# Attention over wide tiles: the next pair's scores issued behind the values instead of ahead of the transposes

## The chip, the cores and the metric

The kernel runs on one NeuronCore of a Trainium2 chip. The metric is the device time of one execution in microseconds (us), lower is better. Three runs of the kernel before took 2337.08, 2338.13 and 2340.18 us; their median, 2338.13 us, is the time before.

## The reference, cut to what matters

One layer of a hybrid block on x of shape (1, 1024, 1024): a norm, an input projection, then two groups of heads side by side (sparse attention with top-k keys, and an mLSTM), an output projection, and a mixture of 32 experts. The change touches only the attention:

```python
idx_score = where(admissible, idx_score, -inf)
_, sel = lax.top_k(idx_score, k_sel)                      # 256 keys of each query
logits = einsum('bqgrd,bqkgd->bqgrk', qb, ks) * scale     # 8 heads of 64, 2 key/value heads
logits = where(valid, logits, -inf)
p = softmax(logits)
out = einsum('bqgrk,bqkgd->bqgrd', p, vs)
```

## The kernel before, in words

Everything before the attention writes what it needs: `q_hi`/`q_lo` and `k_hi`/`k_lo` (float32 split in two parts, so that three fast products replace one exact one), `vtok` (the values) and `score`, which by then holds 0 for a chosen key and a very negative number for every other. The kernel gathers nothing: it computes scores over all keys of the causal prefix and adds that mask.

The attention has 8 tiles of 128 queries. Tile i has w = 128·(i+1) keys, so that tiles 0 to 3 have at most 512 (the constant `NARROW` is 4) and tiles 4 to 7 have 640, 768, 896 and 1024; the text calls the first four narrow and the others wide. Each tile has 8 heads. A unit u is one head of one tile (u = 0 to 63, tile u // 8), and TensorE works on units in pairs u, u+1. For a unit the stages are:

- **scores** (PE, `scores(u)`, L1573 to L1589): one call does both units of a pair; unit u writes PSUM banks 0 and 1 and u+1 banks 2 and 3. It waits until the masks of the preceding pair have read those banks (`v_msk`, L1577).
- **mask** (DVE, L2034 to L2044): adds the mask, copies to `a_s` and takes the row's maximum; L2046 makes the exponential's bias of it.
- **exp** (ACT, L1227 to L1236): exponential of `a_s` into `a_p`, with the row sum.
- **normalize** (DVE, L2007 to L2014): a reciprocal of the sum (L2011) and a multiplication of `a_p` by it (L2014). DVE's own order is mask u, mask u+1, normalize u, normalize u+1 (L2031 to L2049).
- **transposes** (PE, L1631 to L1641): i+1 blocks of `a_p` into PSUM. For narrow tiles the result has a bank for even and one for odd units (L1638); for wide tiles it takes the two banks 4 and 5 together, so that one unit's transposes must have been copied out before the next unit's begin (L1637).
- **copy out** (ACT, `pt_out`, L1238 to L1245): PSUM to `a_t`, which has three slots. ACT's own order is pt_out(u), exp(u+2), pt_out(u+1), exp(u+3) (L1250 to L1253).
- **values** (PE, L1643 to L1653): one call per pair, into banks 6 or 7.

Every engine runs its instructions in the order in which the program gives them. The order on PE is written out by hand in the loop at L1656 to L1665. Four side operations are put between these on ACT and DVE: `q_hi_of` (L1161, ACT, behind exp(u+2) at the third unit of a tile), `q_lo_of` (L2021, DVE, between the masks of the seventh and eighth unit), `mx_hi_of` (L1225, ACT, behind exp(40) and exp(48)) and `mx_lo_of` (L2028, DVE, behind the mask of unit 48). `at_out` (L1054, ACT) copies a finished tile. Behind the attention PE goes on with the output projection (L1431 to L1433).

Of the kernel before, what the change touches and what calls it, by code (L numbers as in the profile page):

```python
# [35 lines left out]
NT = T // P  # L36
# [4 lines left out]
HEADS, HD, KVH = 8, 64, 2  # L41
NARROW = 512 // P
# [299 lines left out]
def build(nc, I, out):  # L342
# [4 lines left out]
    with ExitStack() as ctx:  # L347
# [222 lines left out]
        def pair(b):  # L570

            return ps[:, b:b + 2, :].rearrange("p b n -> p (b n)")
# [27 lines left out]
        def head(u):  # L600

            k = u % HEADS
            return 4 * (k % 2) + k // 2
# [832 lines left out]
        def _(pe):  # L1436
# [136 lines left out]
            def scores(u):  # L1573
                i = u // HEADS
                w = P * (i + 1)
                if u >= 2:
                    pe.wait_ge(s.v_msk, u)  # L1577
                if u % HEADS == 0:
                    pe.wait_ge(s.v_qklo, i + 2)
                for a in range(0, w, 512):  # L1580
                    b = min(a + 512, w)
                    for n, (q_, k_) in enumerate(((q_hi, k_hi), (q_hi, k_lo), (q_lo, k_hi))):
                        for e in range(2):
                            h = head(u + e)
                            rows = slice(HD * (h // 4), HD * (h // 4) + HD)
                            m = nc.tensor.matmul(pair(2 * e)[:, a:b], q_[rows, i % 2, h % 4, :], k_[rows, a:b],
                                                 start=(n == 0), stop=(n == 2))
                            if n == 2 and b == w:
                                m.then_inc(s.p_s, 1)  # L1589
# [41 lines left out]
            def transposes(u):  # L1631
                pe.wait_ge(s.v_arow, u + 1)
                narrow = u // HEADS < NARROW
                if narrow and u >= 2:
                    pe.wait_ge(s.a_pt, u - 1)
                if not narrow:
                    pe.wait_ge(s.a_pt, u)  # L1637
                dst = ps[:, 4 + u % 2, :] if narrow else pair(4)  # L1638
                for j in range(u // HEADS + 1):
                    m = nc.tensor.transpose(dst[:, j * P:(j + 1) * P], a_p[:, u % 2, j * P:(j + 1) * P], ident)  # L1640
                m.then_inc(s.p_pt, 1)  # L1641

            def values(u):  # L1643
                i, j = u // HEADS, u % HEADS // 2
                pe.wait_ge(s.a_pt, u + 2)
                if j == 0 and i >= 2:
                    pe.wait_ge(s.a_at, i - 1)
                for b in range(i + 1):
                    for e in range(KVH):
                        rows = slice(HD * e, HD * e + HD)  # L1650
                        m = nc.tensor.matmul(ps[rows, 6 + i % 2, j * P:(j + 1) * P], vtok[:, b, rows], a_t[:, (u + e) % 3, b, :],  # L1651
                                             start=(b == 0), stop=(b == i), skip_group_check=True)
                m.then_inc(s.p_pv, 1)  # L1653

            pe.wait_ge(s.a_mt, NT)
            for u in range(0, NT * HEADS, 2):  # L1656
                if u + 2 < NT * HEADS:
                    scores(u + 2)
                transposes(u)
                if u // HEADS < NARROW:  # L1660
                    transposes(u + 1)
                if u >= 2:
                    values(u - 2)
                if u // HEADS >= NARROW:
                    transposes(u + 1)  # L1665
            values(NT * HEADS - 2)
            pe.wait_ge(s.g_wolo, 2 * KC)
# [753 lines left out]
```

## Time and profile before

| | |
|---|---|
| median of three runs | 2338.13 us |
| the profiled execution, its own time | 2340.59 us |
| its span in the profile | 2338.8 us |
| PE busy | 2166.9 us (93%) |
| DVE busy | 1836.9 us (79%) |
| ACT busy | 1365.3 us (58%) |
| POOL busy | 560.8 us (24%) |
| mean granted TensorE clock | 0.951 |

The profiled execution is one more run; its own time is 1.8 us over its span, for what lies around it. The attention runs from 513 to 662 us of the span. In timelines, a line is: start, length, engine, line of the kernel, operation, what is written and read, and how often; brackets hold the idle time of the engine before it and the instruction that ended it. Lengths of successive PE lines overlap a little, since matmuls are pipelined; from one start to the next is the real pitch. The granted clock is 1.00 at 2.4 GHz and 0.50 at 1.2 GHz.

### The profile page before, as it was taken

What the parts mean: (1) busy time and instruction counts of PE and PEld (TensorE: products, weight loads), DVE (VectorE), ACT (ScalarE), POOL (GpSimd) and SP (SyncE); (2) the same over time, 40 slices, a digit from 0 to 9 for tenths busy, and PEclk for the clock granted to TensorE, in tenths of its full rate; (3) what the DMA queues carried; (4) which work ended last, traced back from release to release, by engine and by line L of the source; (5) the groups of instructions that cost most, each with busy time, mean ns of one, the idle gap of its engine ahead of it and who ended that gap; (6) DMA issues with size and microseconds to landing.
All of it is one profiled execution on the core that took longest, in us unless ns stands there. A gap on an engine that the chain in (4) does not pass through costs nothing.

```text
span 2338.8 us, 41558 instructions
## 1 busy us (share of the span) xinstructions
PE 2166.9 (93%) x15487; PEld 1731.9 (74%) x15487; DVE 1836.9 (79%) x2152; ACT 1365.3 (58%) x1545; POOL 560.8 (24%) x434
## 2 busy tenths in 40 slices
PE   6899999868899399999999999999999999999994
PEld 5677888645778377778778778778778778778773
DVE  3699999948733767877877877877877877877886
ACT  4542223875742457667667667667667667667665
POOL 1007786665000112112112112112112112112120
PEclk9769999967999699999999999999999999999997
DMA  5011211021023379889889889889889889889897
GB/s 142 19 46 37 55 46 49 29 66 44 1 93 118 105 261 341 311 287 349 309 284 349 310 285 349 313 285 351 309 286 347 313 285 347 311 285 347 315 370 260
DMA packets 253598, 526.46 MB, mean 225 GB/s; under 512 B 33048, under 2 KB 59800, under 8 KB 253180
## 3 DMA queue, kind: packets, MB, share of 16 engines
q1 hardware_dynamic: 240268, 483.27, 57.6%
q0 software_dynamic: 13264, 42.34, 7.5%
q8 instruction: 38, 0.62, 0.1%
q14 instruction: 28, 0.23, 0.0%
HBM read 490.96 MB, written 35.91 MB: 225 GB/s over the span
## 4 chain that ended last, share of the span: by engine, by line
PE 69%; DMA 10%; DVE 9%; ACT 5%; issue 4%; POOL 2%; SPq 0%; DVEq 0%; ACTq 0%; POOLq 0%
PE ps L1763 13%; PE ps L1765 12%; PE ps L1764 12%; DMA e_raw<-in_w_gate_up_dram 9%; PE ps L1770 9%; PE ps L1431 5%; PE ps L1432 5%; PE ps L1433 5%; DVE e_wlo L2262 2%; PE ps L1775 1%; PE ps L1506 1%; PE ps L1651 1%; PE ps L1640 1%; ACT a_p L1235 1%; DVE a_s L2040 1%
## 5 line engine op out<-in xcount | busy, mean ns | idle before, releaser
L1314 ACT ACTIVATE e_whi<-e_raw 128x2048 fp32r<-128x2048 f32 x411 | 785.8, 1917 | 421.5 <-PE ps L1765 313.4
L2262 DVE TENSOR_TENSOR e_wlo<-e_raw,e_whi 128x2048 fp32r<-128x2048 f32 x410 | 926.5, 2284 | 66.9 <-ACT e_whi L1314 65.3
L1763 PE MATMUL ps<-e_whi,xh 128*128 128x512 f32 x1088 | 434.7, 400 | 0.0
L1764 PE MATMUL ps<-e_whi,xl 128*128 128x512 f32 x1088 | 424.3, 390 | 0.0
L1765 PE MATMUL ps<-e_wlo,xh 128*128 128x512 f32 x1088 | 424.1, 390 | 0.0
L942 POOL DMA_INDIRECT x_d<-ym,scur x34 | 73.0, 2146 | 861.9 <-ACT ym L1347 841.5
L1763 PEld LDWEIGHTS ps<-e_whi,xh 128*128 128x128 f32 x1088 | 204.3, 188 | 52.7 <-issue 12.7
L1765 PEld LDWEIGHTS ps<-e_wlo,xh 128*128 128x128 f32 x1088 | 204.2, 188 | 44.0
L1763 PE MATMUL ps<-e_whi,ath 128*128 128x512 f32 x544 | 221.6, 407 | 13.1 <-DVE atl L2290 13.1
L1764 PEld LDWEIGHTS ps<-e_whi,xl 128*128 128x128 f32 x1088 | 204.5, 188 | 39.3
L1765 PE MATMUL ps<-e_wlo,ath 128*128 128x512 f32 x544 | 213.2, 392 | 0.0
L1764 PE MATMUL ps<-e_whi,atl 128*128 128x512 f32 x544 | 212.7, 391 | 0.0
L1431 PE MATMUL ps<-ht_hi,w_hi 128*128 128x512 f32 x416 | 168.8, 406 | 1.2 <-POOL w_lo L793 1.2
L2002 DVE MATCH_REPLACE8 score<-cols,score 128x384 f32<-128x384 f32 (+2 forms) x192 | 166.3, 872 | 0.0
L1433 PE MATMUL ps<-ht_hi,w_lo 128*128 128x512 f32 x416 | 164.3, 395 | 0.0
L1432 PE MATMUL ps<-ht_lo,w_hi 128*128 128x512 f32 x416 | 164.2, 395 | 0.0
L1998 DVE MAX8 cols<-score 128x8 f32<-128x384 f32 (+2 forms) x192 | 160.6, 876 | 0.0
L1763 PEld LDWEIGHTS ps<-e_whi,ath 128*128 128x128 f32 x544 | 102.5, 188 | 52.3 <-issue 33.7
L1770 PE MATMUL ps<-e_raw,xo 128*32 128x128 f32 x4096 | 125.6, 275 | 0.1
L1765 PEld LDWEIGHTS ps<-e_wlo,ath 128*128 128x128 f32 x544 | 102.5, 188 | 22.6
L1764 PEld LDWEIGHTS ps<-e_whi,atl 128*128 128x128 f32 x544 | 102.7, 189 | 18.6
L1770 PEld LDWEIGHTS ps<-e_raw,xo 128*32 128x32 f32 x4096 | 114.5, 111 | 0.6 <-issue 0.3
(351 smaller groups left out, 3348.8 us busy)
## 6 DMA issues: line engine op xcount, KB each, us to landing
e_raw<-in_w_gate_up_dram SPq DMA_DIRECT2D x275, 1024.0 KB, 6.7
e_raw<-in_w_down_dram SPq DMA_DIRECT2D x136, 1024.0 KB, 11.4
w_raw<-in_w_in_dram SPq DMA_DIRECT2D x20, 512.0 KB, 3.8
xt<-in_x_dram SPq DMA_DIRECT2D x8, 512.0 KB, 6.2
xr<-in_x_dram SPq DMA_DIRECT2D x8, 512.0 KB, 4.3
x_d<-x SPq DMA_DIRECT2D x8, 512.0 KB, 2.6
h_d<-h SPq DMA_DIRECT2D x8, 512.0 KB, 2.9
x<-x_d SPq DMA_DIRECT2D x8, 512.0 KB, 7.2
```

The lines of the kernel that those rows point to most:

```text
L942: nc.gpsimd.indirect_dma_start(x2_d[:, :], bass.IndirectOffsetOnAxis(ap=scur[:], axis=0), ym[:], None, compute_op=ALU.add).then_inc(s.st_y ...
L1314: nc.scalar.activation(e_whi[:, m % HRING, :], e_raw[:, m % RING, :], ACT.Copy).then_inc(s.e_hi, 1)
L1431: nc.tensor.matmul(dst, a_hi, b_hi, start=first, stop=False)
L1432: nc.tensor.matmul(dst, a_hi, b_lo, start=False, stop=False)
L1433: return nc.tensor.matmul(dst, a_lo, b_hi, start=False, stop=last)
L1763: nc.tensor.matmul(dst, a_hi, slot_hi, start=False, stop=False, skip_group_check=True)
L1764: nc.tensor.matmul(dst, a_lo, slot_hi, start=False, stop=False, skip_group_check=True)
L1765: return nc.tensor.matmul(dst, a_hi, slot_lo, start=False, stop=last, skip_group_check=True)
L1770: m = nc.tensor.matmul(ps[OVER * b:OVER * b + OVER, bank, 0:n], weights, moving[:, n * b:n * b + n], start=first, stop=last, skip_group_ch ...
L1998: nc.vector.max(top8[:, k, :], sc[k]).then_inc(s.v_topk, 1)
L2002: nc.vector.match_replace(sc[k], top8[:, k, :], sc[k], GONE).then_inc(s.v_topk, 1)
L2262: nc.vector.tensor_tensor(e_wlo[:, m % HRING, :], e_raw[:, m % RING, :], e_whi[:, m % HRING, :].bitcast(F32), ALU.subtract).then_inc(s.e_l ...
```

## The change

In the loop that orders PE's work, for pairs of wide tiles (u = 32 to 62) the call `scores(u + 2)` moves from ahead of `transposes(u)` to behind `values(u - 2)`. For narrow tiles the order stays.

```diff
             for u in range(0, NT * HEADS, 2):
-                if u + 2 < NT * HEADS:
+                narrow = u // HEADS < NARROW
+                if narrow and u + 2 < NT * HEADS:
                     scores(u + 2)
                 transposes(u)
-                if u // HEADS < NARROW:
+                if narrow:
                     transposes(u + 1)
                 if u >= 2:
                     values(u - 2)
-                if u // HEADS >= NARROW:
+                if not narrow and u + 2 < NT * HEADS:
+                    scores(u + 2)
+                if not narrow:
                     transposes(u + 1)
```

No instruction is added or removed, and no other engine's order is touched. The diff is complete.

## Rows read from the trace of the kernel before

**Rows 1.** Busy time by stretch: from, to, length, PE, PEld, DVE, ACT, POOL, PE clock, DMA
```profile
574.00:653.00 79.00, 71.93 (x769) 57.28 (x769) 62.22 (x163) 61.13 (x104) 0.00 (x0) 1.00 0.01 2
```
**Rows 2.** Waits, 574 to 653 us: engine, line, waited for; total us, times, longest
```profile
PE ps L1586 <- DVE cols L2040: 6.4, 10, 1.1
```
**Rows 3.** Timeline of PE, tile 7 (1024 keys), one pair and the next
```profile
648.48 0.50 PE L1586 MATMUL ps<-k_hi,q_hi 64*128 64x512 f32 x2
...
649.74 0.40 PE L1586 MATMUL ps<-k_hi,q_lo 64*128 64x512 f32 x2
650.07 1.09 PE L1640 MATMUL ps<-cst,a_p 128*128 128x128 f32 x8
651.09 1.97 PE L1651 MATMUL ps<-a_t,vtok 128*64 128x128 f32 x32
652.99 1.09 PE L1640 MATMUL ps<-cst,a_p 128*128 128x128 f32 x8
655.29 1.08 PE L1640 MATMUL ps<-cst,a_p 128*128 128x128 f32 x8 [1.21 <-DVE a_p L2014]
```
**Rows 4.** Timeline of DVE and ACT in the same stretch
```profile
651.53 1.22 DVE L2040 CUSTOM_DVE_ANT_0 a_s<-ps,score 128x1024 f32<-128x1024 f32 x1
...
654.13 1.02 ACT L1244 ACTIVATE a_t<-ps 128x1024 f32<-128x1024 f32 x1
```
**Rows 5.** Timeline of PE, tile 4 (640 keys), one pair
```profile
582.79 0.77 PE L1640 MATMUL ps<-cst,a_p 128*128 128x128 f32 x5
583.49 1.31 PE L1651 MATMUL ps<-a_t,vtok 128*64 128x128 f32 x20
584.73 0.76 PE L1640 MATMUL ps<-cst,a_p 128*128 128x128 f32 x5
585.67 0.50 PE L1586 MATMUL ps<-k_hi,q_hi 64*128 64x512 f32 x2 [0.18 <-DVE cols L2040]
...
586.64 0.28 PE L1586 MATMUL ps<-k_hi,q_lo 64*128 64x128 f32 x2
```
**Rows 6.** Timeline of DVE in the same stretch
```profile
583.77 0.82 DVE L2040 CUSTOM_DVE_ANT_0 a_s<-ps,score 128x640 f32<-128x640 f32 x1
...
585.97 0.55 DVE L2014 TENSOR_SCALAR a_p<-a_p,cols 128x640 f32<-128x640 f32 x1
```
**Rows 7.** Timeline of PE, transposes of unit 32, the first wide one
```profile
578.76 0.77 PE L1640 MATMUL ps<-cst,a_p 128*128 128x128 f32 x5
```
**Rows 8.** Timeline of ACT and DVE, one each of the four side operations
```profile
585.65 0.62 ACT L1161 ACTIVATE q_hi<-qt 128x512 fp32r<-128x512 f32 x1
...
589.30 0.68 DVE L2021 TENSOR_TENSOR q_lo<-qt,q_hi 128x512 fp32r<-128x512 f32 x1
...
613.54 1.22 DVE L2028 TENSOR_TENSOR mx_lo<-mixt,mx_hi 128x1024 fp32r<-128x1024 f32 x1
...
614.70 1.04 ACT L1225 ACTIVATE mx_hi<-mixt 128x1024 fp32r<-128x1024 f32 x1
```
**Rows 9.** Timeline of PE in the mLSTM stage, ends of two idle stretches
```profile
447.22 1.16 PE L1618 MATMUL ps<-mvtok,m_w 128*128 128x129 f32 x8 [2.29 <-POOL m_w L837]
...
480.06 1.16 PE L1618 MATMUL ps<-mvtok,m_w 128*128 128x129 f32 x8 [1.30 <-POOL m_w L837]
```
**Rows 10.** Busy time by stretch in the mLSTM stage (the clock is the third number from the end)
```profile
448.00:449.00 1.00, 1.00 (x10) 1.00 (x9) 1.00 (x2) 1.00 (x4) 0.92 (x2) 0.82 0.05 16
...
468.00:469.00 1.00, 0.00 (x0) 0.00 (x0) 1.00 (x2) 1.00 (x5) 1.00 (x1) 1.00 0.00 0
469.00:470.00 1.00, 0.92 (x4) 0.92 (x5) 1.00 (x3) 1.00 (x6) 1.00 (x5) 0.56 0.00 0
...
472.00:473.00 1.00, 1.00 (x9) 1.00 (x8) 1.00 (x3) 0.64 (x5) 1.00 (x2) 0.73 0.00 0
```
**Rows 11.** Timeline of PE, values of tile 2 at the low and the high clock
```profile
559.95 1.55 PE L1651 MATMUL ps<-a_t,vtok 128*64 128x128 f32 x12
...
564.83 0.88 PE L1651 MATMUL ps<-a_t,vtok 128*64 128x128 f32 x12
```

## The prediction

> **What bounds the kernel now.** I began with the page's share of busy time and its 40 slices, to see who is the engine to ask (PE, 93%), then took the busy time by stretch over the wide tiles alone, since the change reaches nothing else. There PE is busy 71.93 of 79 us at the high clock, DVE 62.22 and ACT 61.13 [rows 1]: PE is nearly the bound, the others have some air. The view of waits says what fills PE's idle time: 6.4 us in ten waits of the scores for the masks of the preceding pair [rows 2]. That is all that a better order can win here, and the reader should note how small it is beside what an order can lose.
>
> The timeline of one pair shows why so little is lost. The old order on PE is scores(u+2), transposes(u), values(u-2), transposes(u+1), and round again. The scores of u+2 are issued one whole round before transposes(u+2) need their result. All that lies between (mask, second mask, exponential, reciprocal, normalization) runs beside PE's three other pieces. How long that road is can be read off at the very end of tile 7, where nothing covers it: the first mask starts at 651.53 and the transposes that it feeds at 655.29, released by L2014 [rows 3, 4]. That is M = 3.76 us at 1024 keys. At 640 keys the mask starts at 583.77 and the normalization ends at 585.97 + 0.55 [rows 6], with 0.05 to reach PE (the same as from the end of the transposes, 652.99 + 1.09, to the copy out at 654.13 [rows 3, 4]): M = 2.80 us.
>
> **What the change moves.** Nothing is added or removed, and only PE's queue is re-ordered; the DMA queues, POOL's, ACT's and DVE's stay as they are. The new round is transposes(u), values(u-2), scores(u+2), transposes(u+1), transposes(u+2). Between the scores and the transposes that need them there is now one piece, transposes(u+1), of 0.76 to 1.09 us [rows 3, 5]. The road of 2.80 to 3.76 us is no longer covered. So PE stands in front of transposes(u+2) in every round, and the whole round becomes a serial chain: transposes(u), values(u-2), scores(u+2), mask, exponential, normalization, transposes(u+2). What is queued behind the waiting instruction is values(u) and scores(u+4), and these are what DVE and ACT wait for: no engine can run ahead.
>
> A second wait comes due at the same moment. Transposes(u+2) also need banks 4 and 5, so pt_out(u+1), which in ACT's order stands behind exp(u+2). In tile 7 that copy ends at 654.13 + 1.02 = 655.15 [rows 4], 0.14 before the transposes start. Both roads pass exp(u+2) and end almost together, so the second adds nothing by itself; it matters for the side operations below.
>
> **The length of a round**, by the starts of successive pieces. Tile 7: transposes 651.09 - 650.07 = 1.02; values 652.99 - 651.09 = 1.90; scores to their end 649.74 + 0.40 - 648.48 = 1.66; 0.05; M 3.76: sum 8.39 us [rows 3, 4]. Tile 4: 583.49 - 582.79 = 0.70; 584.73 - 583.49 = 1.24; 586.64 + 0.28 - 585.67 = 1.25; 0.05; 2.80: sum 6.04 us [rows 5, 6]. Each piece grows with the number of keys, so I take the tiles between in equal steps: 6.82 and 7.61 us. From transposes(32) to transposes(62) there are 15 rounds, four each of tiles 4 to 6 and three of tile 7: 4·(6.04 + 6.82 + 7.61) + 3·8.39 = 107.1 us. (Rounds on the border of two tiles mix their widths; that cancels within 0.2 us.) Before, the same 15 rounds ran from 578.76 to 655.29 [rows 3, 7], 76.5 us. **Term one: +30.6 us.** What comes behind transposes(62) has no scores in it in either order and stays.
>
> **Term two, the side operations.** ACT's and DVE's extras now fall on the chain. q_hi stands between exp and pt_out, three times 0.62 less the 0.14 of slack: 1.4 us. q_lo stands between the two masks and delays the normalization, three times some 0.6 of its 0.68: 1.8. mx_hi before transposes(40) costs 1.0 of its 1.04; before transposes(48) mx_hi and mx_lo are late side by side, so the longer counts, 1.2 [rows 8]. Sum +5.4 us. Part of it was already in the 76.5, but as new rounds replace old ones it is added to the new sum in full.
>
> Ends: scores(34) no longer stand ahead of transposes(32), which may start up to 1.2 us earlier, if they don't wait for their own normalization; I take 0. Unchanged clock: 30.6 + 5.4 = **+36 us**. Bounds: if the roads overlap better than read, term two could be 0 and the shift 1.2 (+29); if each round has 0.3 us more of hand-overs, +41.
>
> **Term three, the clock.** PE's new idle stretch in each round is its length less its pieces: 6.04 - 0.70 - 1.24 - 1.25 - 0.76 = 2.1 us in tile 4, and 8.39 - 1.02 - 1.90 - 1.66 - 1.09 = 2.7 in tile 7. In all of the wide tiles so far no wait of the scores exceeds 1.1 us, and the clock stays at 1.00 (2.4 GHz) [rows 1, 2]. The trace has idle stretches of the new size in the mLSTM stage. After 2.29 us of idle to 447.22 the clock fell within 448 to 449 (0.82); after PE stood still through 468 to 469 it fell early in 469 to 470 (0.56), to the 1.2 GHz level; after 1.30 us to 480.06 it did not fall [rows 9, 10]. The fall of 469 lasted until the clock rose in 472 to 473 (0.73): (0.56 - 0.50)/0.50 = 0.12 of the first and 0.46 of the last microsecond were high, so 3.4 us were low, with PE busy again [rows 10]. The same 12 value matmuls take 1.55 us low and 0.88 high [rows 11]. So a fall costs 3.4·(1 - 0.88/1.55) = 1.5 us of PE's time, and transposes, values and scores are all on the chain now. With 15 idle stretches of 2.1 to 2.7 us I take 13 falls: **+19 us**. The ends are no fall (0) and a clock low throughout: transposes, values and scores of a round, 3.2 to 4.6 us, times 1.55/0.88 - 1 = 0.76, which is 2.4 to 3.5, some 3.0 on average, times 15: +44 us.
>
> A page speaks against this term. The Trainium skill, "TensorE: Matmul & The Clock Gate", section "Why this matters for your kernels", asks for no idle gaps of more than about 3 us between bursts; ours are shorter, so by that rule the clock would hold and the sum stop at +36. By the two falls in the rows, after shorter gaps than that, it is +55. The same page, under "A second HAM failure mode: psum-queue depth-cycling", tells of a kernel whose short but frequent idles made the clock go up and down; that speaks for the term. I go by the rows.
>
> **The sum.** 2340.59 + 36 + 19 = 2395.6 us against the profiled execution, which was 2.46 over the median; against the median 2393 us.
>
> **The rivals.**
> - Forecast: serial chain, clock falling once in most rounds. 2393 us, its own range 2383 to 2405. Chance 0.55.
> - The chain with a steady clock (falls need longer gaps, or the bursts of over 4 us between them keep it up): 2338.1 + 36 = 2374 us. For it: 79 us of wide tiles at 1.00; against it: rows 9 and 10. 0.20.
> - The chain with the clock low nearly throughout: 2338.1 + 36 + 44 = 2418 us. For it: the low clock cost rows 11 their time in the narrow tiles with PE in work; against it: in rows 10 it rose again while PE was dense, and the new rounds have 4 to 5 us of that. 0.12.
> - Only the copy out is uncovered: transposes(u+2) find their normalization done and wait for pt_out alone, 0.9 to 1.2 us by the width, 15 times, 16 us, less the 6.4 of waits for masks that go and 1.2 at the end: +8, 2346 us. It needs exp(u+2) to be done before transposes(u+1) end, and the masks can't start before the scores. 0.06.
> - The other side: the masks get values' time as cover, PE's waits for them (6.4) and the last for L2014 (1.21) go and nothing comes instead: 2338.1 - 7.6 = 2330.5 us. The mechanism is the wait before the scores, whose place is L1577; it decides if the road M fits under transposes(u+1), so below 1.09 us. It is 2.80 at the least. 0.04.
> - Gain and new wait cancel: 0.03.
>
> That the change does not do what it says can't be: the order is written out.
>
> **The numbers.** The likeliest case gives 2393. Range 2370 to 2414: it takes in the steady clock and the lower part of the third case, and leaves out some 2 in 10 (the small or absent losses, and a clock low all the time). A measurement of this kernel can tell about 0.2%, 4.7 us, from no change. Faster 0.04, same 0.03, slower 0.93.
>
> **What would show it.** In the new timeline PE should stand 2 to 3 us in front of the first transposes of each pair, ended by DVE's L2014 or ACT's L1244, and the scores should never wait for L2040. DVE should idle before mask u+2, ended by PE's L1586. A round in tile 7 should take 8.4 us or more. The granted clock by stretch should dip under 1.00 several times between 578 and 690 us. The prediction is wrong if rounds stay near 5.5 us, or if the idle is there and the clock never moves (then 2374).

## The result and the profile after

The changed kernel takes 2387.34 us (median of four runs, 2386.95 to 2391.91) against 2337.91 us for the kernel before. The ratio is 1.0212, with a 95% interval of 1.0200 to 1.0225: 49.4 us slower. The profiled execution took 2391.91 us, 51.3 more than that of before. Forecast were 2393 us and a range of 2370 to 2414.

The page of the changed kernel, its first lines and the granted clock in 40 slices:

```profile
span 2390.1 us, 41558 instructions
...
PE 2184.6 (91%) x15487; PEld 1746.8 (73%) x15487; DVE 1839.1 (77%) x2152; ACT 1365.9 (57%) x1545; POOL 553.6 (23%) x434
...
PEclk8779999867889879999999999999999999999997
```

As many instructions as before, and busy times of DVE and ACT within 3 us of before: the time is waiting, not work. PE's busy time grew by 18 us although it executes the same matmuls, which fits a lower clock. The eleventh and twelfth slice, 597 to 717 us, lie in the wide tiles and show 8, where they showed 9 before.

The busy time by stretch over the wide tiles, which answers to [rows 1]:

```profile
578.00:705.00 127.00, 83.98 (x757) 67.94 (x753) 63.56 (x160) 61.61 (x103) 0.00 (x0) 0.88 0.00 1
```

PE is busy 66% where it was 91%, at a mean clock of 0.88 where it was 1.00.

The view of waits of the changed kernel, 578 to 712 us, which answers to [rows 2] (waiter, waited for; total us, times, longest):

```profile
DVE a_s L2043 <- PE ps L1586: 47.7, 15, 4.6
...
PE ps L1640 <- DVE a_p L2017: 31.4, 12, 3.7
...
PE ps L1640 <- ACT a_t L1244: 11.6, 4, 3.2
```

(The diff moves DVE's lines by three: L2043 is the mask, L2017 the normalization.) The scores' waits for the masks, 6.4 us before, are gone. In their place PE waits 43 us in front of the transposes, and DVE waits 47.7 us for scores, which it never had to in the wide tiles before. Every engine waits for another in turn: that is what a serial chain looks like in this view. PE's waits that end with the normalization (31.4 of 43 us) also rule out the rival in which only the copy out is uncovered.

One round in tile 7, PE and then DVE and ACT, which answers to [rows 3] and [rows 4]:

```profile
686.64 1.09 PE L1640 MATMUL ps<-cst,a_p 128*128 128x128 f32 x8 [2.76 <-DVE a_p L2017]
...
687.66 1.97 PE L1651 MATMUL ps<-a_t,vtok 128*64 128x128 f32 x32
...
689.56 0.50 PE L1586 MATMUL ps<-k_hi,q_hi 64*128 64x512 f32 x2
...
691.14 1.09 PE L1640 MATMUL ps<-cst,a_p 128*128 128x128 f32 x8
691.25 1.23 DVE L2043 CUSTOM_DVE_ANT_0 a_s<-ps,score 128x1024 f32<-128x1024 f32 x1 [2.64 <-PE ps L1586]
...
693.85 1.00 ACT L1244 ACTIVATE a_t<-ps 128x1024 f32<-128x1024 f32 x1
...
695.00 1.55 PE L1640 MATMUL ps<-cst,a_p 128*128 128x128 f32 x8 [2.77 <-DVE a_p L2017]
```

From transposes to transposes this round takes 8.36 us (forecast: 8.39). From the mask to the transposes it feeds are 3.75 us (M was read as 3.76), and the copy out ends at 694.85, 0.15 before them. PE stands 2.77 us. Over the 15 rounds of the wide tiles these idle stretches are 2.15 to 3.69 us long; forecast were 2.1 to 2.7, from rounds without side operations.

What a fall of the clock does is seen in tile 4. The timeline of PE has the same 20 value matmuls twice, at the low clock (2.40 us) and at the high one (1.31 us). The busy time by stretch has the granted clock around the first (third number from the end):

```profile
585.62 0.76 PE L1640 MATMUL ps<-cst,a_p 128*128 128x128 f32 x5 [2.15 <-DVE a_p L2017]
586.31 2.40 PE L1651 MATMUL ps<-a_t,vtok 128*64 128x128 f32 x20
...
602.12 1.31 PE L1651 MATMUL ps<-a_t,vtok 128*64 128x128 f32 x20
```

```profile
584.00:586.00 2.00, 0.38 (x3) 0.39 (x4) 1.49 (x5) 2.00 (x5) 0.00 (x0) 1.00 0.02 4
586.00:588.00 2.00, 2.00 (x20) 1.83 (x20) 0.72 (x2) 0.89 (x3) 0.00 (x0) 0.57 0.04 8
588.00:590.00 2.00, 2.00 (x18) 1.43 (x14) 0.00 (x0) 0.00 (x0) 0.00 (x0) 0.58 0.00 0
590.00:592.00 2.00, 1.05 (x13) 0.74 (x9) 1.58 (x4) 0.56 (x1) 0.00 (x0) 1.00 0.00 0
```

After an idle stretch of 2.15 us the clock goes to the 1.2 GHz level when PE has its burst to do, and comes back in the last part of it. Counted in stretches of 1 us, the clock fell ten times between 578 and 714 us and was low for 3.4 us each time. Eight falls began with PE's burst. Two began in the wait before it, such as this one, where PE executes nothing until 631.04:

```profile
630.00:631.00 1.00, 0.00 (x0) 0.00 (x0) 0.92 (x5) 1.00 (x2) 0.00 (x0) 0.82 0.00 0
```

### The profile page after: what moved, and what is told of

Its sections match the earlier page's. It is cut to its first block, busy times and chain, and to the rows that moved or that the text cites. A ratio compares the mean times of both kernels' runs of the same rounds, so it can differ in the third digit from the quotient of the medians.

```text
span 2390.1 us, 41558 instructions
## 1 busy us (share of the span) xinstructions
PE 2184.6 (91%) x15487; PEld 1746.8 (73%) x15487; DVE 1839.1 (77%) x2152; ACT 1365.9 (57%) x1545; POOL 553.6 (23%) x434
## 4 chain that ended last, share of the span: by engine, by line
PE 69%; DVE 10%; DMA 10%; ACT 4%; issue 4%; POOL 2%; SPq 0%; DVEq 0%; ACTq 0%; POOLq 0%
PE ps L1766 13%; PE ps L1768 12%; PE ps L1767 12%; DMA e_raw<-in_w_gate_up_dram 9%; PE ps L1773 8%; PE ps L1431 5%; PE ps L1432 5%; PE ps L1433 5%; PE ps L1651 2%; DVE e_wlo L2265 2%; DVE a_s L2043 1%; PE ps L1778 1%; PE ps L1506 1%; PE ps L1586 1%; PE ps L1640 1%
## 5 line engine op out<-in xcount | busy, mean ns | idle before, releaser
L1766 PE MATMUL ps<-e_whi,ath 128*128 128x512 f32 x544 | 221.8, 408 | 13.4 <-DVE atl L2293 13.4
```

The lines of the kernel that those rows point to most:

```text
L1766: nc.tensor.matmul(dst, a_hi, slot_hi, start=False, stop=False, skip_group_check=True)
```

## The experiments

Medians are of four to eleven runs; each ratio is against runs of the kernel before on the same chip, whose median was 2339.47 us for fill12, fill12_side, mid and dve_order, and 2338.62 us for the other four. "The 15 rounds" are from the start of transposes(32) to that of transposes(62) in each kernel's profile: 76.5 us in the kernel before, 579.80 to 705.00 = 125.2 us in the changed one.

**Filling PE's idle time.** In front of the first transposes of each wide pair, float32 products whose result the values later overwrite (they are done beside the computation, which stays whole):

```diff
+            def fill(u, n):
+                i, j = u // HEADS, u % HEADS // 2
+                if j == 0:
+                    pe.wait_ge(s.a_at, i - 1)
+                for _ in range(n):
+                    nc.tensor.matmul(ps[:, 6 + i % 2, j * P:(j + 1) * P], const("ones"), const("ones"), start=True, stop=True,
+                                     skip_group_check=True)
...
                 if not narrow:
                     transposes(u + 1)
+                    if u + 2 < NT * HEADS:
+                        fill(u, 12)
```

> The changed kernel with 12 extra float32 products of 128 columns (results overwritten later) in front of the first transposes of each wide pair, where PE now waits. They leave the output alone and should fit the wait: 12 at some 0.12 us are 1.4 us, the waits are 2.1 to 2.8 us. Theory (serial chain plus clock falls): the chain is not longer and the clock stays at 1.00 from 578 to 690 us, so the time falls by nine or ten falls at 1.5 us, to about 2374 us. Rival (the whole loss is the chain, the low clock costs nothing since the engine waits anyway): no gain, 2387 us or a little over. Second rival (the extra products stand in the way): over 2390 us.

Measured: 2372.82 us, ratio 1.0135 (1.0118 to 1.0151). The busy time by stretch, then one filled gap in the timeline of PE:

```profile
574.00:640.00 66.00, 63.13 (x647) 56.09 (x644) 38.07 (x103) 35.85 (x66) 0.00 (x0) 1.00 0.01 1
640.00:694.00 54.00, 52.21 (x535) 45.51 (x533) 29.10 (x65) 28.89 (x44) 0.00 (x0) 1.00 0.01 2
```

```profile
586.83 0.77 PE L1640 MATMUL ps<-cst,a_p 128*128 128x128 f32 x5
587.44 2.84 PE L1660 MATMUL ps<-cst 128*128 128x128 f32 x24
590.17 0.73 PE L1640 MATMUL ps<-cst,a_p 128*128 128x128 f32 x5
```

Giving PE useless work made the kernel 14.5 us faster by the medians, and 16 by the losses against the kernel before in each call (49.4 and 33.4). From 574 to 694 us the clock stayed at 1.00, and the 15 rounds take 577.60 to 689.38 = 111.8 us, 13.4 less than in the changed kernel, which has nine of its ten falls in these rounds. The rival that the low clock costs nothing has fallen. What is left, 111.8 - 76.5 = 35.3 us, is the chain with a steady clock. One detail was mis-sized: a product takes 0.23 us and not 0.12, so that in tile 4 the twelve fill the whole gap and stand a little in the way (0.35 us in the first round).

**Half of the fill**, `fill(u, 6)`:

> As fill12 with 6 extra products. Measured there: one takes 0.23 us (24 records, 2.84 us for 12), so that 12 fill all of the 2.1 us in tile 4 and some of them were on the chain (rounds of 6.2 us where the changed kernel's rounds without a fall have 5.8). Six take 1.4 us and leave 0.7 to 1.4 us of idle. Theory (the clock holds if the idle is short, and the fill is then off the chain): clock 1.00, transposes(32) to transposes(62) in 110 to 112.5 us against 111.8 for fill12, 1 to 2 us less in all: 2371 to 2372 us. Rival (six are not enough to keep the clock up): falls come back, 2375 to 2387 us.

Measured: 2374.65 us, ratio 1.0153 (1.0138 to 1.0169), 15 rounds in 112.9 us. Both are over what the theory gave. The timeline shows part of the reason: one fall remained, after the one idle stretch that is still long (2.35 us, the others are at most 1.89), where `mx_lo` lies on the chain. Without its 1.6 us the 15 rounds would take 111.3 us, inside the range given. The fall:

```profile
632.12 0.98 PE L1640 MATMUL ps<-cst,a_p 128*128 128x128 f32 x7 [2.35 <-DVE a_p L2027]
633.03 2.45 PE L1651 MATMUL ps<-a_t,vtok 128*64 128x128 f32 x24
```

The same round, transposes(48) to transposes(50), takes 632.12 to 641.03 = 8.91 us here and 633.06 to 640.39 = 7.33 us with twelve products and no fall: 1.58 us.

The other rounds give the strongest evidence of this study. The six rounds of the changed kernel that have no fall last as long as the same rounds here within 0.02 us each (5.82 and 5.82 us for the first, 8.36 and 8.37 in tile 7). So six products stand in nobody's way, and the whole difference lies in the rounds with a fall. There are nine. Compared one by one with the same round here (the one behind transposes(48) with twelve products), they are 1.36 to 1.62 us longer, 13.9 us in sum. The two cheapest, 1.36 and 1.40, are those in which the clock fell while PE still waited: some 0.4 to 0.5 us of their low time fell on an idle PE. Without the falls the 15 rounds take 125.2 - 13.9 = 111.3 us.

**The side operations off the chain**, with either fill:

```diff
-                if u % HEADS == 2 and u // HEADS + 1 < NT:
+                if u % HEADS == (2 if u < NARROW * HEADS else 3) and u // HEADS + 1 < NT:
                     q_hi_of(u // HEADS + 1)
...
-                if u in (4 * HEADS + 6, 5 * HEADS + 6):
+                if u in (4 * HEADS + 7, 5 * HEADS + 7):
                     mx_hi_of(u // HEADS - 4)
```

> As fill12, and for wide tiles q_hi_of and the two mx_hi_of one unit later in ACT's order, behind exp of an odd unit, where ACT has time. Theory (copy out of the odd unit's transposes ends just with the normalization, so whatever ACT does between exp(u+2) and that copy is on the chain): three times 0.5 and once 1.0 us less, 2.5 us under fill12, and the waits of L1640 that end with L1244 go. Rival (the side operations lie beside the chain): the same as fill12 within 0.5 us.

> As fill6, with q_hi_of and mx_hi_of one unit later on ACT. With the smaller fill nothing hides what they cost: theory 2.0 to 2.5 us less than fill6 between transposes(32) and transposes(62). With 12 fills it was 1.6. Rival (side operations are beside the chain and 1.6 was scatter): the same as fill6 within 0.5 us.

Measured: 2370.91 us (1.0134, 1.0119 to 1.0150) and 2373.97 us (1.0151, 1.0136 to 1.0167). The 15 rounds take 577.84 to 688.04 = 110.2 us with twelve products and 577.95 to 688.89 = 110.9 with six, so 1.6 and 2.0 us less than without the edit, where 2.5 and 2.0 to 2.5 were expected. The medians of the whole program differ by 1.9 and 0.7 us, which their scatter covers. Of PE's waits in fill12, the two that ended with the copy out are gone. The longer is this one, at transposes(40), where ACT has `mx_hi` and then the copy out:

```profile
602.06 1.04 ACT L1225 ACTIVATE mx_hi<-mixt 128x1024 fp32r<-128x1024 f32 x1
603.00 0.68 ACT L1244 ACTIVATE a_t<-ps 128x640 f32<-128x640 f32 x1
603.83 0.85 PE L1640 MATMUL ps<-cst,a_p 128*128 128x128 f32 x6 [0.56 <-ACT a_t L1244]
```

So ACT's extras are on the chain, as read from the trace of before, at some 2 us in the profiles; the medians alone would not show it. At transposes(48) the edit changed nothing: with six products the idle stretch is 2.36 us and the clock falls once, as without it. What holds the chain there is `mx_lo` on DVE, which stayed in its place.

**One place earlier.** The scores between transposes(u) and values(u-2):

```diff
                 transposes(u)
                 if narrow:
                     transposes(u + 1)
+                if not narrow and u + 2 < NT * HEADS:
+                    scores(u + 2)
                 if u >= 2:
                     values(u - 2)
-                if not narrow and u + 2 < NT * HEADS:
-                    scores(u + 2)
                 if not narrow:
                     transposes(u + 1)
```

> The changed kernel with the scores of wide pairs one place earlier: transposes(u), scores(u+2), values(u-2), transposes(u+1). Theory (what counts is how much PE work stands between the scores and the transposes that use them): values now cover part of the road, a round is transposes + scores + 0.05 + M, 4.8 us at 640 keys and 6.5 at 1024, 15 rounds 83.8 and the side operations 5.4, so 12.7 us over the kernel before: 2351 us, with idle stretches under 1.2 us and no clock falls. Rival (the loss comes from banks 4 and 5, because transposes(u+1) and transposes(u+2) now follow each other with the copy out between): the same neighbours as in the changed kernel, so its loss stays, 2374 to 2387 us.

Measured: 2354.69 us, ratio 1.0067 (1.0052 to 1.0083), so 15.2 us over the kernel before of the same call. The 15 rounds take 578.44 to 668.22 = 89.8 us; the theory's sum was 83.8 + 5.4 = 89.2. The clock stayed at 1.00 as expected, though the idle stretches did not stay under 1.2 us: ten of the 15 are longer, up to 2.23. The timeline of PE in tile 7:

```profile
659.15 1.09 PE L1640 MATMUL ps<-cst,a_p 128*128 128x128 f32 x8
661.45 1.07 PE L1640 MATMUL ps<-cst,a_p 128*128 128x128 f32 x8 [1.21 <-ACT a_t L1244]
```

The transposes of two units are neighbours here just as in the changed kernel, with the one copy out between them, and the loss is 15 us instead of 49 (of which some 15 us are falls of the clock, as the fill showed). So it is not the neighbours but the amount of PE work behind the scores that sets the loss: with transposes(u+1) alone +49, with values and transposes(u+1) +15, with all three pieces 0. In tile 7 the wait that ends last is the copy out, and its rounds of 6.8 us are 0.3 over the sum: of the two roads the one that I had left out of this sum wins there, by little.

**DVE's order, on the kernel before.**

```diff
-                if u % 2 == 1:
+                late = u >= NARROW * HEADS
+                if u % 2 == 1:
                     normalize(u - 1)
-                    normalize(u)
+                    if not late or u + 1 == NT * HEADS:
+                        normalize(u)
+                elif u >= NARROW * HEADS + 2:
+                    normalize(u - 1)
```

> The kernel BEFORE with only DVE's order changed for wide tiles: mask u+2, normalize u+1, mask u+3, normalize u+2, so that DVE masks while ACT still computes the exponential that normalize u+1 needs. Theory (PE's 6.4 us of waits for masks come from DVE standing before that normalization, 14.6 us in all): masks end earlier, PE runs without a wait, up to 6 us less than before: 2332 to 2336 us. Rival (PE is the bound already and its waits are only moved, now in front of transposes(u+1), whose normalization comes later): 2338 us, or up to 5 us more.

Measured: 2332.64 us, ratio 0.9971 (0.9961 to 0.9980): 6.8 us faster than the kernel before, and better than both kernels of this study. Its waits from 574 to 648 us:

```profile
PE ps L1586 <- DVE cols L2040: 2.3, 4, 1.2
```

Of the 6.4 us of [rows 2] 4.1 are gone, and the wait of DVE for the exponential, 14.6 us before, is down to one of 1.7 at the end. The 15 rounds take 577.07 to 648.59 = 71.5 us, 5.0 less than before. In the profiles this kernel is 1.7 us earlier already ahead of the wide tiles, where the edit does nothing, so some 5 of the 6.8 us are the order's.

**The same order of DVE on the changed kernel:**

> The CHANGED kernel with the DVE order of dve_order (mask u+2, normalize u+1, mask u+3, normalize u+2). That edit took 7 us off the kernel before. Theory (in the changed order the road from the scores to the transposes is the chain, and a normalization more stands on it between the two masks): each of 15 rounds gets 0.7 to 0.9 us longer, and the idle stretches too, so more falls: 12 us or more on 2387, 2397 to 2408 us. Rival (DVE's order helps wherever PE waits for DVE): under 2387 us.

Measured: 2413.87 us, ratio 1.0316 (1.0299 to 1.0332), 26.5 us over the changed kernel. The edit that gains 7 us with the scores ahead loses 26 with the scores behind, so the rival is out. But the loss is over the range given (2397 to 2408 us), and the timeline shows two things that the sum lacked. The lines are from the border of tiles 5 and 6:

```profile
648.03 1.12 PE L1640 MATMUL ps<-cst,a_p 128*128 128x128 f32 x6 [2.11 <-DVE a_p L2017]
...
649.27 0.79 ACT L1244 ACTIVATE a_t<-ps 128x768 f32<-128x768 f32 x1
...
651.15 1.75 PE L1640 MATMUL ps<-cst,a_p 128*128 128x128 f32 x7 [2.00 <-DVE a_p L2017]
```

PE now waits twice in a round: normalize u+1 stands behind mask u+2, so transposes(u+1) are late as well, and with them the copy out that the next transposes need. (The second wait is 2.00 us here, where `mx_lo` and `mx_hi` add to it; in the other rounds it is 0.89 to 1.61.) And the clock is low far longer: it fell 14 times up to the end of the attention, and often stayed low for twice the 3.4 us or more, so that it was low for some 85 us, where it was low for 34 in the changed kernel. The only round with a steady clock, transposes(32) to (34), grew from 5.82 to 6.39 us, and all 15 from 125.2 to 576.61 to 727.07 = 150.5 us. If every round had grown by 0.6 us, that would be 9 of the 25 us, and the clock would have the rest; this is an estimate from one round, and no run divides the two.

**Side operations, with the better order:** the two edits above on the kernel before, together.

> dve_order with q_hi_of and mx_hi_of one unit later on ACT. With the scores ahead, PE's work covers the road, so by the theory the side operations are beside it and their place is worth under 1 us either way: 2331 to 2334 us. Rival (they are on the chain there too): 2 us or more less than dve_order.

Measured: 2333.59 us, ratio 0.9978 (0.9969 to 0.9987), against 0.9971 for DVE's order alone: no difference, as expected where PE's work covers ACT's.

## Why the prediction was right, and where it was off

**What bounds the kernel now**: right. The 6.4 us that an order could win went, and were small beside what it lost.

**What the change moves**: right. The experiment mid and the changed kernel (without the falls) show the mechanism at two lengths of cover, near the sum worked out from the old trace (89.8 for 89.2, and 111.3 to 111.8 for 112.5). In mid there is some luck in that: the copy out, which its sum left out, ends seven of the 15 waits.

**Term one and two, the chain**: forecast +30.6 and +5.4, so 112.5 us for the 15 rounds; without the falls they took 111.3 (13.9 us for the falls by the rounds) to 111.8 (fill12). The trace of fill6_side has, for each tile, a round with neither a side operation nor a fall: 583.77 to 589.80 = 6.03, 609.23 to 615.97 = 6.74, 640.37 to 647.91 = 7.54 and 672.15 to 680.52 = 8.37 us, for 6.04, 6.82, 7.61 and 8.39. So the two middle tiles, taken in equal steps, were 0.1 too long, and the rest is as read. The 1.6 to 2.0 us of ACT's part of term two are a little under the 2.4 that I had counted for it (1.4 for `q_hi` and 1.0 for `mx_hi`). DVE's part was not tried by itself, but in the same trace the rounds of tiles 4 to 6 in which `q_lo` stands between the masks are longer than those by 0.45, 0.48 and 0.52 us, where I had 0.6 each. Transposes(32) came 0.3 us earlier relative to the work ahead of them, where I took 0: they wait for their own normalization.

**Term three, the clock**: the mechanism was right and its size was off. The price of a fall was read as 1.5 us; measured are 1.36 to 1.62 us round by round. Their number is what was mis-sized: I took 13 falls in 15 idle stretches, without a reason for 13 rather than another number, and the profile has ten, one of them behind transposes(62). So the term is 13.4 to 13.9 us in the rounds, and 8.64 us instead of 7.01 for what follows transposes(62) to the output projection, together some 15 us instead of 19. The 51.3 us between the two profiled executions are 48.7 in the rounds, 1.6 behind them, less the 0.3 above, and 1.3 that the changed kernel was later already ahead of the wide tiles, where the change does nothing. The three other runs of the changed kernel are another 4 to 5 us lower, at a mean clock of 0.946 to 0.947 instead of 0.940 over the execution. Fewer falls might do that, but those runs have no timeline to count them in, and the mean clock is no guide: in runs of the kernel before it lies between 0.945 and 0.953 and the time does not follow it (2336.14 us at 0.949, 2341.04 at 0.952).

**The page against the term.** I had weighed a rule of the Trainium skill ("TensorE: Matmul & The Clock Gate", section "Why this matters for your kernels"), no idle gaps over about 3 us, and had written that all of ours are shorter. Four of the 15 are not (3.04, 3.05, 3.24 and 3.69 us). The trace does not agree with the rule in either direction: eight of the ten falls came with gaps under 3 us, from 2.15 us on (at 585.62), and the clock held after those of 3.04 and 3.24. Going by the rows was right.

**The rivals**: a steady clock is out by the ten falls, a clock low throughout by the returns after each, the copy out alone by the waits (12 of 16 end with the normalization) and by mid, the gain and the cancelling by the sign.

## What to carry to other kernels

In an order written by hand, ask for each producer how much work of its own engine stands between it and its first consumer, and compare that with the road over the other engines, read where the trace shows it uncovered (here, at the end of the last tile). If the cover is shorter, the difference comes back in every round, and no wait in the old trace announces it. An idle PE can cost more than its idle time: in the changed kernel ten of 15 idle stretches of over 2 us brought a fall of the clock, at some 1.5 us each.

## What was not expected of the hardware

The length of the idle stretch alone does not decide on a fall. The clock fell after 2.15 us and did not after 3.24 us, both in the changed kernel:

```profile
608.62 0.84 PE L1640 MATMUL ps<-cst,a_p 128*128 128x128 f32 x6 [3.24 <-ACT a_t L1244]
```

In tile 7 the same wait of 2.76 us brought a fall at 705.00 and none at 686.64. In mid waits of 1.99 and 2.23 us left the clock at 1.00 too. With DVE's order on the changed kernel shorter waits were enough, two in a round: the clock fell in 583 to 584 us behind these two.

```profile
581.34 0.77 PE L1640 MATMUL ps<-cst,a_p 128*128 128x128 f32 x5 [1.77 <-DVE a_p L2017]
583.00 0.73 PE L1640 MATMUL ps<-cst,a_p 128*128 128x128 f32 x5 [0.89 <-DVE a_p L2017]
```

What decides was not tried.
